# A recurrence's score products, in front of the levels or one at a time between them

## What is computed

```python
def wkv7_scan(S0, inputs, reverse):
    xs = tuple(jnp.swapaxes(t.astype(jnp.float32), 0, 1) for t in inputs)

    def step(S, inp):
        r, w, k, v, kk, a = inp
        S = (S * w[:, :, None, :]
             - jnp.einsum('bhvk,bhk->bhv', S, kk)[..., None] * (kk * a)[:, :, None, :]
             + v[..., None] * k[:, :, None, :])
        return S, jnp.einsum('bhvk,bhk->bhv', S, r)

    S, y = lax.scan(step, S0, xs, reverse=reverse)
    return S, jnp.swapaxes(y, 0, 1)
...
    S_cf, y_cf = wkv7_scan(S0, dir_inputs(f_ctx, 0), reverse=False)
    S_cb, y_cb = wkv7_scan(S0, dir_inputs(f_ctx, 1), reverse=True)
    _, y_lf = wkv7_scan(S_cf, dir_inputs(f_lat, 0), reverse=False)
    _, y_lb = wkv7_scan(S_cb, dir_inputs(f_lat, 1), reverse=True)
```

## Time and profile before

| | |
|---|---|
| median of 3 runs | 2828.0 us (2827.4 to 2834.32) |
| the profiled execution | 2829.54 us, its span 2827.8 us |
| TensorE matmuls | 2536.1 us busy, 90% of the span |
| VectorE | 1515.0 us, 54% |
| ScalarE | 891.9 us, 32% |
| mean granted TensorE clock | 0.951 |
| `wkv` on TensorE | from about 1235.8 to 1476 us of the span |

### The profile page before, as it was taken

One profiled execution on the slowest core, in us unless ns is written; L12 is line 12 of the kernel. 1 busy time (PEld: TensorE's weight loads), 2 busy tenths in 40 slices (PEclk: granted clock), 3 DMA queues, 4 the chain that ended last, 5 costly groups with the idle time before them and its releaser, 6 DMA issues.

```text
span 2827.8 us, 41887 instructions
## 1 busy us (share of the span) xinstructions
PE 2536.1 (90%) x17518; PEld 2006.7 (71%) x17518; DVE 1515.0 (54%) x2517; ACT 891.9 (32%) x1547; POOL 76.5 (3%) x148
## 2 busy tenths in 40 slices
PE   8999999799997899548886899998999997888998
PEld 6687778588875567248773588876788875556998
DVE  5656475555554655674543555545555543664554
ACT  2331131422222333712220422223322223343543
POOL 0000000000000000000000000000000000000000
PEclk9999999999998999779998999999999998999999
DMA  7235436243433110000011243443344441101553
GB/s 285 82 118 200 172 121 220 99 142 135 148 134 136 60 45 31 0 2 4 4 39 52 84 147 137 141 149 119 129 139 142 142 143 69 43 30 45 175 184 134
DMA packets 55770, 309.72 MB, mean 110 GB/s; under 512 B 5920, under 2 KB 9376, under 8 KB 28064
## 3 DMA queue, kind: packets, MB, share of 16 engines
q1 hardware_dynamic: 32944, 224.74, 22.2%
q0 software_dynamic: 20736, 75.51, 8.0%
q10 hardware_dynamic: 1904, 6.80, 0.6%
HBM read 305.98 MB, written 1.05 MB: 109 GB/s over the span
## 4 chain that ended last, share of the span: by engine, by line
PEld 39%; PE 31%; issue 12%; DVE 11%; ACT 7%; DMA 1%; PEldq 0%; DVEq 0%; ACTq 0%; SPq 0%
PEld bank L1206 13%; PEld bank L1199 13%; PEld bank L1202 12%; PE bank L1079 4%; PE bank L1258 4%; PE bank L1076 2%; PE bank L1052 2%; PE bank L1138 2%; PE bank L1154 2%; PE bank L943 2%; PE bank L950 2%; PE bank L946 2%; ACT hn L1567 2%; PEld bank L910 1%; PE bank L1033 1%
## 5 line engine op out<-in xcount | busy, mean ns | idle before, releaser
L1991 DVE TENSOR_TENSOR w_lo<-ring,w_hi 128x1024 fp32r<-128x1024 f32 (+1 forms) x198 | 236.2, 1193 | 450.6 <-ACT w_hi L1532 450.6
L1202 PE MATMUL bank<-ffn_x_lo,w_hi 128*128 128x512 f32 x1008 | 399.6, 396 | 0.0
L1206 PE MATMUL bank<-ffn_x_hi,w_lo 128*128 128x512 f32 x1008 | 399.6, 396 | 0.0
L1199 PE MATMUL bank<-ffn_x_hi,w_hi 128*128 128x512 f32 x1008 | 399.6, 396 | 0.0
L1532 ACT ACTIVATE w_hi<-ring 128x1024 fp32r<-128x1024 f32 (+1 forms) x198 | 203.7, 1029 | 290.2 <-PE bank L1202 278.6
L1923 DVE SCALAR_TENSOR_TENSOR ms<-mod_rows,c_silu 128x1024 f32<-128x1024 f32 x200 | 243.9, 1220 | 1.2
L1206 PEld LDWEIGHTS bank<-ffn_x_hi,w_lo 128*128 128x128 f32 x1008 | 189.9, 188 | 46.3
L1199 PEld LDWEIGHTS bank<-ffn_x_hi,w_hi 128*128 128x128 f32 x1008 | 189.9, 188 | 46.3
L1202 PEld LDWEIGHTS bank<-ffn_x_lo,w_hi 128*128 128x128 f32 x1008 | 189.8, 188 | 46.3
L1199 PE MATMUL bank<-ffn_h_hi,w_hi 128*128 128x512 f32 x528 | 211.7, 401 | 0.0
L1206 PE MATMUL bank<-ffn_h_hi,w_lo 128*128 128x512 f32 x528 | 209.3, 396 | 0.0
(11 more groups left out here) (430 smaller groups left out, 4642.8 us busy)
## 6 DMA issues: line engine op xcount, KB each, us to landing
ring<-in_stream SPq DMA_DIRECT2D x211, 1024.0 KB, 4.8
mod_rows<-in_mod_stream POOLq DMA_DIRECT2D x144, 512.0 KB, 3.8
one_const<-in_one ACTq DMA_DIRECT2D x1, 1665.0 KB, 14.2
mix_const<-in_two ACTq DMA_DIRECT2D x1, 1440.0 KB, 6.2
win_const<-in_win ACTq DMA_DIRECT2D x1, 1089.0 KB, 5.4
x<-in_x SPq DMA_DIRECT2D x4, 256.0 KB, 4.5
c_silu<-in_c SPq DMA_DIRECT2D x1, 1024.0 KB, 10.3
x<-in_x SPq DMA_DIRECT2D x1, 1024.0 KB, 26.5
```

The lines of the kernel that those rows point to most:

```text
L1199: mm = pe.matmul(bank[:, 0:tok], w_high, hi, start=k == 0, stop=False)
L1202: mm = pe.matmul(bank[:, 0:tok], w_high, lo, start=False, stop=False)
L1206: mm = pe.matmul(bank[:, 0:tok], w_low, hi, start=False, stop=last)
L1991: V.tensor_tensor(low[:, 0:h.nk, :], raw_half(h), high[:, 0:h.nk, :].bitcast(F32), ALU.subtract).then_inc(sem("w_split"), 1)
```

## The change

In `wkv_order`'s `prepare` the four products of kinds 1 and 2 no longer stand in front of the levels. One of them comes between the inner and the outer product of each of the first four levels. The other engines follow, since all read the same order. The code of the steps is the same.

```diff
             def prepare(i):
                 yield ("tokens", i)
-                for k in range(3):
-                    for nth in range(2):
-                        yield ("products", i, k, nth)
+                for nth in range(2):
+                    yield ("products", i, 0, nth)
                 for lvl in range(1, LEVELS):
-                    for what in ("inner", "outer"):
-                        yield (what, i, lvl)
+                    yield ("inner", i, lvl)
+                    if lvl < LEVELS - 1:
+                        yield ("products", i, 1 + (lvl - 1) // 2, (lvl - 1) % 2)
+                    yield ("outer", i, lvl)
```

## The result

The changed kernel takes **2840.7 us** (median of 9 runs, 2831.9 to 2845.0) against 2830.7 us for the kernel before (median of 9 runs beside it): a ratio of 1.0032, 95% interval 1.0020 to 1.0044. So it is slower by 10 us, by about the least that can be told from no change, and outside the range of the prediction (2823 to 2839). The profiled executions are 2841.0 us (span 2839.2) and 2829.5 us (span 2827.8), 11.5 us apart.

A forecast was written before the change was run, and what follows sets the result against it. TensorE, busy 90%, bounds the kernel; its one large hole waits for VectorE behind the masks. Three recurrence parts (+0.9 us) plus the first preparation (+1.5) give +2.4 on 2828.0: 2830.5 us, range 2823 to 2839.

The forecast's parts named there:

- (e): In each part with a recurrence, TensorE's pauses that no engine releases: forecast 0, with -0.5 to +1.0 us a part.
- 12 moved steps of 1 us each: Slower rival: each of twelve moved steps with a recurrence brings a 1 us pause, +12 us, 2842 us; chance 0.04.
- (a): The first level's inner product now waits for VectorE's masks ahead of recurrence steps: +0.9 us a part.
- (b): Inner product's wait for the preceding outer product's subtraction, 0.34 us lost: two of four go, -0.7 us a part.
- (c): VectorE's evictions of moved products, now ahead of a level's subtraction: hidden by outer products; up to 5.1 us a part uncovered.
- (d): Clock falls in the wait for the masks as before; restart costs the same 1.9 us, so 0; bounds -1.9 and +3.5.
- The rival in which it stays low through the first level: Slower rival: longer idle keeps the clock low through the first level in four preparations, 15 us, 2846 us; chance 0.09.
- The first preparation: Block 0's preparation, without recurrence: moved products no longer hide behind mask work, +1.5 us; it grows to 44 to 46 us.
- y0's wait gone: TensorE's wait for VectorE's bank release before the recurrence's first y step, 3.94 us in the middle part, disappears.
- the two waits of I1: First level's inner product waits twice for VectorE, 5 to 6 us then over 2 us, in each part and first preparation.
- the 0.34 us of I2 and I4: Inner products of levels 2 and 4 lose their 0.34 us wait because a recurrence step now precedes each.
- one sooner rise: Range's lower end: the clock is not low when TensorE's dense run behind the wait begins, -1.9 us.

The follow-up runs named there:

- few-instruction runs: Products of kinds 1 and 2 replaced by fewer, wider matmuls on zero blocks in both kernels: 2831.7 us in the changed order, 2829.0 us in the old one.

## Why the prediction was wrong

**(e) is the step that failed: the pauses without a releaser.** I took 0 a part with +1.0 as the upper end. They cost 6.5 us over three parts, 2.2 a part. The text had both halves of the answer. It saw that the pauses of 1.08 and 1.47 us cost nothing where they were, as y0 waited for VectorE anyway, and it listed 12 moved steps of 1 us each as a rival, 2842 us, which is within 1.3 us of the result. That nearness is partly luck, as the pauses brought 6.5 us and not 12. It gave that rival 0.04 for the reason that the steps are spread among level work, issued at half the rate. That reason fell: the pauses don't need three products in a row, and their sum was 8.8 us in the one order and 8.2 in the other. A product among the levels was enough for one of 0.8 to 0.9 us in the first part (1313.6, 1325.9, 1333.5); in the second part of the same kernel none was over 0.4. Carried over as they were, the 7.1 us that lay in the shadow would have been 2.4 us a part, near the 2.2 measured. With 6.5 us in place of 0, the prediction's own sum gives 2830.5 + 6.5 = 2837.0 us. Of the 3.7 us that are left to 2840.7, 2.7 are the base: the forecast was added to 2828.0, a median of three runs, and nine runs gave 2830.7. By that base the upper end of the range would have been 2841.7. So that the time lies outside the range is owed to the base too; that the change is +10.1 and not +2.4 is owed to (e) first. The few-instruction runs show that it is this term: with the same 20.3 us of waits for the masks, the pauses fell to 3.5 us and the two orders came to 2.7 us from one another, near the +2.4 of the sum without (e).

**(a) held.** The first half of I1 starts behind a wait of 5.49 us and the second behind 1.45. The text had over 2 us for the second, since it let the first half take 0.95; at the low clock it takes 1.97, inside the same wait. The second half starts 16.2 us behind x0 (1298.97 - 1282.74); the forecast had 1353.4, which is 16.0 us behind the x0 at 1337.4. In the first preparation the two waits are 4.1 and 1.4 us, less than the 5 to 6 and over 2 named. VectorE's last mask rows after confirm who is late:

```profile
1294.66 0.68 DVE L2409 SCALAR_TENSOR_TENSOR rstd<-rstd,mix_const 128x512 f32<-128x512 f32 x1
...
1298.08 0.69 DVE L2409 SCALAR_TENSOR_TENSOR mod_rows<-mod_rows,mix_const 128x512 f32<-128x512 f32 x1
```

**(b) held**: I2 (from 1310.0) and I4 (from 1330.2) run from the first to the last matmul in 1.9 us with no gap between the directions, while I3 and I5 keep theirs of about 0.35. Together (a), (b) and small rests leave 8.9 - 6.5 = 2.4 us in three parts, where +0.9 was forecast. What the other 1.5 us are was not found.

**(c) held**: in the view of waits none of TensorE's ends on L2417, where the evictions of the moved products free their banks, or on a level's subtraction.

**(d) held in the parts.** The low clock covers the second half of I1 and s0 (1299.0 to 1302.7, 3.7 us of dense work) instead of y0 (4.1), and y0 runs at full clock from 1307.8 in 2.2 us. The rows of 2 us (clock third last):

```profile
1300.00:1302.00 2.00, 2.00 (x69) 2.00 (x70) 0.69 (x1) 0.60 (x1) 0.00 (x0) 0.50 0.00 0
1302.00:1304.00 2.00, 2.00 (x108) 2.00 (x101) 0.99 (x3) 0.00 (x0) 0.00 (x0) 0.83 0.04 8
```

The rival in which it stays low through the first level is out: O1 begins at 1303.5 and by 1304 the clock is at 1.00; in the third part it is so from 1425.6, in the first microsecond of O1.

**The first preparation** grew by 2.7 us in the profile where +1.5 was forecast. The 44 to 46 us named go by the cut of the earlier trace rows, by which it is 46.1 (43.8 to x0). A pause of 0.77 us in front of x0 and a low clock over 5.3 us of dense work (1249.6 to 1254.9) are the likely rest, but one order of steps alone spreads by 3.5 us there (40.2 to 43.7), so this term is not settled to a microsecond. Block 0 in its old order gave back 1.5 us of the median, which is within the scatter.

**Of the signs named beforehand**, y0's wait gone, the two waits of I1, the clock over I1 and s0, and the 0.34 us of I2 and I4 came as said. "The parts keep 56 to 59 us" did not (59.7 to 61.4), and that is (e). Of the three things that would have shown the forecast wrong, none came: s0 did not start before I1, no part fell below 55.5 us, and y0 ran at full clock. They looked for a gain or the clock, not for pauses. The lower end of the range was also mis-added: one sooner rise (-1.9) and -0.5 in three parts are -3.4, and -6 to -7 needs the sooner rise in every part.

## What to carry over

A pause costs nothing while it stands in front of a wait that ends later anyway, and its full length once its step is moved behind it: price a moved step with the pauses that it has in the trace, not with its work alone. Fill a long wait with what needs nothing from the late engine (here y0 and s0: 12 us gained by the medians), and leave in it the densest steps, beside which the pauses lie (moving kind 2 out gained 6.8 us, moving kind 1 out as well turned that into a loss of 10). A queue's transfers set beside the pauses, in slices of a microsecond, tell such pauses from waits.

## What the runs showed of the hardware

- TensorE paused for 0.2 to 1.8 us without a releaser where small fp32 matmuls come close together. In the kernels before and after these pauses end 2.2 to 2.9 us behind the start of a 16384-byte transfer of instructions. Such a transfer holds 256 instructions. In the dense work of 1300 to 1340 they start 3.4 to 4.5 us apart; while the engine waited for VectorE none started (1288.3 to 1300.0). That the transfer is late, and not merely beside the pause, is argued from this timing and from the few-instruction runs, and not shown.
- In the old order the pauses in front of a wait for VectorE cost next to nothing: with stand-ins of fewer instructions all pauses fell from 8.8 us to 1.5, and the waits for VectorE grew from 12.2 to 18.9 us.
- An empty instruction with a semaphore increment took 0.16 us on TensorE.
- A fp32 matmul of 384 columns of a 128x128 matrix took about 0.65 us at full clock (14 in 9.2 us, 6 in 4.0).
- With the clock held at 1.00 through the hole (y0 in 2.2 us, not 4.1) it fell to 0.50 later, in dense work, in two of three parts (3.4 us each), and the pauses among the levels went from 1.7 to 3.4 us. The kernel was no faster.
